# Sparse attention: the low parts of a finished pair one query block later on VectorE

## The chip, the cores and the metric

One core of a Trainium2 chip runs the whole program in one launch. The metric is the device time of that launch in microseconds (us); lower is better.

## The reference, cut to what matters

The reference is a chain of two transformer blocks over 512 tokens of width 1024. Nearly all of it stays out of this case. What matters is the mixer of the last layer, an attention of 12 heads (4 groups of 3) over 512 queries, with three branches that share the queries: over 31 compressed keys, over selected blocks of keys, and over a window. With 512 tokens all blocks are selected and the window covers all earlier keys, so that the two fine branches are causal attentions with their own keys and values:

```python
s_c = einsum('bgrqd,bgkd->bgrqk', qb, kc) + common_bias(d_c)
o_c = einsum('bgrqk,bgkd->bgrqd', masked_softmax(s_c, d_c >= 0), vc)
...
o = gb[..., 0:1] * o_c + gb[..., 1:2] * o_s + gb[..., 2:3] * o_w
...
h = h + jnp.concatenate([main, mo], axis=-1) @ w_out[i]
```

The kernel computes the dense products in fp32 from two parts of each operand: an upper part, rounded to the type that TensorE multiplies at full rate, and a low part, the rest. For the output projection (`@ w_out`), the attention's result is needed as xH (upper) and xL (low).

## The kernel before, in words

**Stages.** Each engine runs a hand-written list of stages in a fixed order: projections, the attention (`attend_pe`, `attend_dve`, `attend_act`), then the output projection `nsa_out` and the last feed-forward layer. Engines meet through counting semaphores alone.

**Pairs and blocks.** The 12 heads are worked off as 6 pairs. `items` (line 2467) lists 30 blocks: for each pair the coarse block over the compressed keys (t None), then the query blocks t = 0 to 3 of 128 queries, whose scores have 128(t + 1) columns. A block of t = 0 to 3 has two branches of two heads.

**The loop.** All three engines run m = 0 to 32, and each takes other blocks in one round:
- TensorE (`attend_pe`, L2553): the scores of block m (`scores_pe`; L2497 coarse, L2509 fine), which first wait until VectorE has the maxima of block m - 1 (`n_raw`); the turning (transposition, L881) of block m - 2, first branch; the product with the values of block m - 3 (`out_pe`, L2540 coarse, L2548 fine); the turning of the second branch.
- VectorE (`attend_dve`, L2643): the maxima of block m (`max_dve`: L2583 to L2592 coarse, L2600 and L2606 fine), which wait for the scores branch by branch; the scaling of block m - 1 (`scale_dve`, L2625 to L2639), which waits for its exponentials; and, when block m - 3 was the last of its pair, the low parts of that pair (`rest_dve`).
- ScalarE (`attend_act`, L2694): the copy of the turned block m - 2 (L2692), the exponentials of block m (`exp_act`, L2678), and, when block m - 3 was the last of its pair, the pair's upper parts (`upper_act`, L2712), which wait for all five products of the pair (`n_out`).

**The pair's result.** `out_pe` adds all five blocks of a pair up in one PSUM bank, bank 7 for even pairs and bank 2 for odd ones. `upper_act` copies its two halves (64 rows by 512 each) to xH and signals `x_hi`; `rest_dve` waits for that, subtracts xH from the bank into xL (L2659) and signals `x_ready`. `x_ready` is read by the coarse product of the pair after the next (L2538), which reuses the bank, and by `nsa_out`.

**The order on VectorE.** With the last block of a pair at index 5p + 4, the low parts stand in round 5p + 7: after the maxima of the next pair's block 1 and the scaling of its block 0, ahead of the maxima of its block 2. For the last pair this is round 32, where nothing else is left.

**Tables.** GpSimd loads the bias table of a later pair when `n_raw` tells that a pair's maxima are done (L2371). TensorE's clock is not set by the program.

Of the kernel before, what the change touches and what calls it, by code (L numbers as in the profile page):

```python
# [134 lines left out]
def build(nc, A, out):  # L135

    with ExitStack() as ctx:
        sems = {}

        def sem(name):  # L140
            if name not in sems:
                sems[name] = ctx.enter_context(nc.semaphore(name))
            return sems[name]
# [186 lines left out]
        def xbase(f):  # L330
            return sum(XFILL[:f])
# [1569 lines left out]
        def mem_out_dve(dve, l, base, place, hi):  # L1901

            dve.wait_ge(sem("m_out"), NROUND * (l + 1))
            for j in range(2):
                dve.wait_ge(sem("x_hi"), base + j + 1)
                nc.vector.tensor_tensor(place[:, j, :], bank[2 + j][:], hi[:, j, :], ALU.subtract)\
                  .then_inc(sem("x_ready"), 1)
# [558 lines left out]
        NPAIR = AH // 2  # L2466
        items = [(p, t) for p in range(NPAIR) for t in (None, 0, 1, 2, 3)]
# [3 lines left out]
        def pair_head(p, u):  # L2471

            return p + 3 * (p // 3) + 3 * u

        def lower_upper(half):

            return slice(64 * half, 64 * half + 64)
# [5 lines left out]
        def out_bank(p):  # L2483

            return bank[7 if p % 2 == 0 else 2]
# [157 lines left out]
        def attend_dve(dve):  # L2643
            for m in range(len(items) + 3):
                if m < len(items):
                    max_dve(dve, m)
                if m == 0:
                    mem_out_dve(dve, 1, xbase(9), xL[:, 6:8, :], xHf[:, 6:8, :])
                if 1 <= m <= len(items):
                    scale_dve(dve, m - 1)  # L2650
                if m >= 3 and items[m - 3][1] == 3:
                    rest_dve(dve, items[m - 3][0])

        def rest_dve(dve, p):
            for u in range(2):
                h = pair_head(p, u)
                f = lower_upper(h % 2)
                dve.wait_ge(sem("x_hi"), xbase(9) + 2 + 2 * p + u + 1)
                nc.vector.tensor_tensor(xL[f, h // 2, :], out_bank(p)[f, :], xHf[f, h // 2, :], ALU.subtract)\  # L2659
                  .then_inc(sem("x_ready"), 1)  # L2660
# [310 lines left out]
        def _(dve):  # L2971
# [74 lines left out]
            for k in range(KD):  # L3046
# [3 lines left out]
            dense_dve(dve, "nsa_q", evac_scaled(aq_place, rstd[:]),  # L3050
                      extra={(0, r): lambda r=r: mem_round_dve(dve, 1, r) for r in range(NROUND)})
            attend_dve(dve)
            dense_dve(dve, "nsa_out", residual(1.0))
            for k in range(KD):
# [65 lines left out]
```

## Time and profile before

| | |
|---|---|
| Time, median of 3 runs | 2518.57 us (2516.82 to 2520.32) |
| The profiled execution: its own time | 2519.59 us |
| its span, first to last instruction | 2517.8 us |
| Mean granted TensorE clock | 0.983 |
| Busy: TensorE matmul, VectorE, ScalarE, GpSimd | 97%, 53%, 38%, 6% of the span |
| DMA | 215.80 MB, mean 86 GB/s |

The profile is one execution. PE is TensorE's matmuls, PEld its weight loads, DVE is VectorE, ACT is ScalarE, POOL is GpSimd, SP is SyncE. A row of a timeline gives the start from the span's start and the length in us, the engine, the line of the kernel, the operation, what it writes and reads, and how many instructions are merged in it; in brackets stands the idle time of the engine before it and what ended that. The granted clock is a share of TensorE's full clock of 2.4 GHz. The ends of matmuls are modelled, so their starts are the firmer numbers.

### The profile page before, as it was taken

Reading aid. Unit: us, or ns where it says so; the run is one execution under the profiler, and the core shown is the slowest. Engines: PE = TensorE matmul, PEld = TensorE weight load, DVE = VectorE, ACT = ScalarE, POOL = GpSimd, SP = SyncE. Lnnn points to the kernel's source line nnn. Section 1 sums busy time; section 2 is a strip of 40 time slices with the busy share of each in tenths; the row PEclk is TensorE's granted clock in tenths of the full one; section 3 lists DMA queues with packets and bytes.
Section 4 is the critical chain, followed back from the end, with each engine's and each line's share of the span. In section 5 each row is a group of like instructions: output and inputs, shape, how many; then the busy total and the mean of one; then the engine's idle time right before and its main releaser. Section 6 shows DMA issues by size and latency. Waiting matters only on the chain.

```text
span 2517.8 us, 32093 instructions
## 1 busy us (share of the span) xinstructions
PE 2429.9 (97%) x12218; PEld 1972.6 (78%) x12218; DVE 1338.9 (53%) x2054; ACT 960.4 (38%) x1461; POOL 151.8 (6%) x130
## 2 busy tenths in 40 slices
PE   7999998998999999999899999999999888999999
PEld 6888886778878888887887788878887557888887
DVE  4344336665454343345785766643534873666633
ACT  4222226632243223235333533432324773433323
POOL 3000001013011000021000100000110000000001
PEclk9999999999999999999999999999999999999999
DMA  4333222220123332223122233332844102333322
GB/s 138 96 96 100 92 86 74 71 72 10 51 68 100 96 95 92 92 85 84 44 66 76 76 99 93 92 100 93 168 122 121 45 16 67 92 99 93 100 92 76
DMA packets 319121, 215.80 MB, mean 86 GB/s; under 512 B 49289, under 2 KB 302748, under 8 KB 319016
## 3 DMA queue, kind: packets, MB, share of 16 engines
q1 hardware_dynamic: 315752, 200.40, 27.7%
q0 software_dynamic: 3264, 13.94, 1.6%
q8 instruction: 72, 1.18, 0.2%
q14 instruction: 33, 0.27, 0.0%
HBM read 212.17 MB, written 8.44 MB: 88 GB/s over the span
## 4 chain that ended last, share of the span: by engine, by line
PE 85%; DVE 7%; ACT 5%; issue 2%; DMA 0%; POOL 0%; POOLq 0%; ACTq 0%; DVEq 0%
PE bank L521 17%; PE bank L522 16%; PE bank L523 16%; PE bank L708 6%; PE bank L707 6%; PE bank L706 6%; PE bank L881 1%; DVE wL L426 1%; DVE arena L2600 1%; ACT wH L390 1%; PE bank L2087 1%; PE bank L1569 1%; PE bank L2509 1%; PE bank L1583 1%; PE bank L1578 1%
## 5 line engine op out<-in xcount | busy, mean ns | idle before, releaser
L521 PE MATMUL bank<-xH,wH 128*128 128x512 f32 x1960 | 783.2, 400 | 21.0 <-DVE xL L780 10.0
L523 PE MATMUL bank<-xH,wL 128*128 128x512 f32 x1960 | 769.6, 393 | 0.0
L522 PE MATMUL bank<-xL,wH 128*128 128x512 f32 x1960 | 769.1, 392 | 0.0
L426 DVE TENSOR_TENSOR wL<-raw,wH 128x1024 fp32r<-128x1024 f32 (+1 forms) x359 | 449.5, 1252 | 535.4 <-ACT wH L390 534.9
L390 ACT ACTIVATE wH<-raw 128x1024 fp32r<-128x1024 f32 (+1 forms) x359 | 376.0, 1048 | 758.1 <-PE bank L523 342.8
L521 PEld LDWEIGHTS bank<-xH,wH 128*128 128x128 f32 x1960 | 369.4, 188 | 120.2 <-issue 27.9
L522 PEld LDWEIGHTS bank<-xL,wH 128*128 128x128 f32 x1960 | 369.9, 189 | 81.1 <-issue 4.8
L523 PEld LDWEIGHTS bank<-xH,wL 128*128 128x128 f32 x1960 | 369.2, 188 | 81.1 <-issue 1.0
L708 PE MATMUL bank<-g_hi,wL 128*128 128x512 f32 x704 | 280.9, 399 | 0.0
L706 PE MATMUL bank<-g_hi,wH 128*128 128x512 f32 x704 | 276.3, 393 | 1.2 <-DVE wL L426 1.2
L707 PE MATMUL bank<-g_lo,wH 128*128 128x512 f32 x704 | 277.4, 394 | 0.0
L2217 ACT ACTIVATE arena<-arena,par 128x512 f32<-128x512 f32 x88 | 63.6, 725 | 270.1 <-DVE arena L2249 270.1
L707 PEld LDWEIGHTS bank<-g_lo,wH 128*128 128x128 f32 x704 | 132.1, 188 | 34.1
L706 PEld LDWEIGHTS bank<-g_hi,wH 128*128 128x128 f32 x704 | 132.2, 188 | 34.0 <-DVE wL L426 2.5
L708 PEld LDWEIGHTS bank<-g_hi,wL 128*128 128x128 f32 x704 | 132.2, 188 | 30.5
L2249 DVE TENSOR_TENSOR arena<-bank,rstd 128x512 f32<-128x512 f32 x88 | 60.6, 691 | 86.6 <-PE bank L523 81.0
L733 ACT ACTIVATE arena<-arena 128x512 f32<-128x512 f32 x44 | 27.6, 631 | 173.8 <-DVE arena L740 173.8
L827 POOL TENSOR_TENSOR rstd<-sq 128x512 f32<-128x512 f32 x7 | 10.2, 1453 | 1290.7 <-ACT sq L790 1290.7
L742 DVE TENSOR_TENSOR arena<-bank,rstd 128x512 f32 (+1 forms) x44 | 30.3, 691 | 103.3 <-PE bank L523 103.3
L881 PEld LDWEIGHTS bank<-ident,arena 128*128 128x128 f32 (+3 forms) x402 | 46.0, 145 | 48.5 <-issue 34.7
L881 PE MATMUL bank<-ident,arena 128*128 128x128 f32 (+3 forms) x402 | 61.0, 292 | 22.8 <-DMA arena<-in_x 9.3
L740 DVE TENSOR_TENSOR arena<-bank,rstd 128x512 f32<-128x512 f32 x44 | 30.2, 691 | 85.6 <-PE bank L523 80.1
(337 smaller groups left out, 2679.0 us busy)
## 6 DMA issues: line engine op xcount, KB each, us to landing
raw<-in_ffn_w_in SPq DMA_DIRECT2D x88, 512.0 KB, 3.8
raw<-in_w_up SPq DMA_DIRECT2D x88, 512.0 KB, 3.8
raw<-in_ffn_w_out SPq DMA_DIRECT2D x44, 512.0 KB, 3.4
raw<-in_w_down SPq DMA_DIRECT2D x44, 512.0 KB, 3.5
raw<-in_w_mix_in SPq DMA_DIRECT2D x28, 512.0 KB, 3.8
raw<-in_w_kv_shared SPq DMA_DIRECT2D x12, 512.0 KB, 8.3
rel_wide<-rel_rows POOLq DMA_DIRECT2D x12, 512.0 KB, 10.9
arena<-rel_wide POOLq DMA_DIRECT2D x12, 448.0 KB, 4.2
```

The source lines that it names most:

```text
L390: nc.scalar.activation(wH[:, half_slot(s, i, j), 0:n], raw[:, k, 0:n], ACT.Copy).then_inc(sem("w_hi"), 1)
L426: nc.vector.tensor_tensor(wL[:, h, 0:n], raw[:, k, 0:n], wH[:, h, 0:n].bitcast(F32), ALU.subtract)\
L521: pe.matmul(o, wh, xa, start=a, stop=False)
L522: pe.matmul(o, wh, xb, start=False, stop=False)
L523: last = pe.matmul(o, wl, xa, start=False, stop=z)
L706: pe.matmul(bank[m][:], wh, gh, start=f == 0, stop=False)
L707: pe.matmul(bank[m][:], wh, gl, start=False, stop=False)
L708: last = pe.matmul(bank[m][:], wl, gh, start=False, stop=f == NF - 1)
L742: nc.vector.tensor_tensor(g[:, bass.ds(2 * i + t - 2, 1), :], one(bank[t][:]), one(rstd[:]), ALU.mult)\
L881: return pe.transpose(o, i, ident[0:k, 0:k])
L2217: nc.scalar.activation(cv[:, t, :], us[:, t, :], ACT.Copy, scale=conv_columns(s, i, t)[2])\
L2249: nc.vector.tensor_tensor(us[:, t, :], bank[t][:], rstd[:], ALU.mult).then_inc(sem("evac_dve"), 1)
```

## The change

The pair's low parts are made one round later: in round 5p + 8, that is after the maxima of the next pair's block 2 (its third fine block) and the scaling of its block 1, ahead of the maxima of its block 3. The last pair's low parts move behind the loop, where they follow the same instruction as before. No instruction, wait or signal is added or taken away.

```diff
--- before.py
+++ after.py
@@ -2648,8 +2648,9 @@
                     mem_out_dve(dve, 1, xbase(9), xL[:, 6:8, :], xHf[:, 6:8, :])
                 if 1 <= m <= len(items):
                     scale_dve(dve, m - 1)
-                if m >= 3 and items[m - 3][1] == 3:
-                    rest_dve(dve, items[m - 3][0])
+                if m >= 4 and items[m - 4][1] == 3:
+                    rest_dve(dve, items[m - 4][0])
+            rest_dve(dve, NPAIR - 1)
 
         def rest_dve(dve, p):
             for u in range(2):
```

## Rows read from the trace of the kernel before

**Rows 1.** Page, busy time of each engine, and the chain by engine.

```profile
PE 2429.9 (97%) x12218; PEld 1972.6 (78%) x12218; DVE 1338.9 (53%) x2054; ACT 960.4 (38%) x1461; POOL 151.8 (6%) x130
PE 85%; DVE 7%; ACT 5%; issue 2%; DMA 0%; POOL 0%; POOLq 0%; ACTq 0%; DVEq 0%
```

**Rows 2.** Attention stage: length, busy PE, PEld, DVE, ACT, POOL, PEclk, DMA, GB/s.

```profile
1942.00:2089.30 147.30, 123.07 (x1065) 82.06 (x1065) 112.20 (x459) 103.95 (x319) 4.48 (x9) 0.92 0.10 32
```

**Rows 3.** Waits, 1935 to 2092 us: total, times, longest.

```profile
DVE xL L2659 <- ACT xH L2712: 14.1, 6, 7.0
DVE arena L2600 <- PE bank L2509: 14.0, 13, 2.0
```

**Rows 4.** Timeline, low parts: start, length, engine, line, tiles [idle before, releaser].

```profile
2019.69 1.41 DVE L2659 TENSOR_TENSOR xL<-bank,xH 64x512 fp32r<-64x512 f32 x2 [1.37 <-ACT xH L2712]
...
2087.54 1.41 DVE L2659 TENSOR_TENSOR xL<-bank,xH 64x512 fp32r<-64x512 f32 x2 [7.01 <-ACT xH L2712]
```

**Rows 5.** Timeline of the third such place, PE and DVE.

```profile
2014.37 1.13 PE L2509 MATMUL bank<-arena 64*128 64x256 f32 x8
...
2015.26 0.42 DVE L2600 CUSTOM_DVE_ANT_0 arena<-bank,arena 128x256 f32<-128x256 f32 x1 [1.99 <-PE bank L2509]
...
2018.32 1.56 PE L2509 MATMUL bank<-arena 64*128 64x384 f32 x8
...
2021.13 0.56 DVE L2600 CUSTOM_DVE_ANT_0 arena<-bank,arena 128x384 f32<-128x384 f32 x1
2021.19 0.44 PE L881 MATMUL bank<-ident,arena 128*128 128x128 f32 x2
...
2023.19 3.38 PE L2509 MATMUL bank<-arena 64*128 64x512 f32 x8 [1.56 <-DVE col L2600]
...
2025.45 0.69 DVE L2600 CUSTOM_DVE_ANT_0 arena<-bank,arena 128x512 f32<-128x512 f32 x1 [0.46 <-PE bank L2509]
```

**Rows 6.** Timeline of DVE, waits in the maxima of block 3, other places.

```profile
1980.74 0.69 DVE L2600 CUSTOM_DVE_ANT_0 arena<-bank,arena 128x512 f32<-128x512 f32 x1 [0.16 <-PE bank L2509]
...
2048.60 0.69 DVE L2600 CUSTOM_DVE_ANT_0 arena<-bank,arena 128x512 f32<-128x512 f32 x1 [0.38 <-PE bank L2509]
...
2050.14 0.69 DVE L2600 CUSTOM_DVE_ANT_0 arena<-bank,arena 128x512 f32<-128x512 f32 x1 [0.23 <-PE bank L2509]
...
2073.20 0.69 DVE L2600 CUSTOM_DVE_ANT_0 arena<-bank,arena 128x512 f32<-128x512 f32 x1 [0.26 <-PE bank L2509]
```

**Rows 7.** Timeline round the coarse scores, pair 0 to 1, then 3 to 4.

```profile
1960.27 0.62 DVE L2583 TENSOR_TENSOR arena<-bank,arena 128x124 f32<-128x124 f32 x2
1960.40 0.88 PE L881 MATMUL bank<-ident,arena 128*128 128x128 f32 x6 [1.12 <-DVE arena L2639]
...
1969.63 0.43 DVE L2600 CUSTOM_DVE_ANT_0 arena<-bank,arena 128x256 f32<-128x256 f32 x1 [1.81 <-PE bank L2509]
...
2028.26 1.08 PE L2497 MATMUL bank<-arena 64*128 64x31 f32 x16
...
2030.10 0.62 DVE L2583 TENSOR_TENSOR arena<-bank,arena 128x124 f32<-128x124 f32 x2
2030.24 0.88 PE L881 MATMUL bank<-ident,arena 128*128 128x128 f32 x6 [0.90 <-DVE arena L2639]
...
2038.48 0.43 DVE L2600 CUSTOM_DVE_ANT_0 arena<-bank,arena 128x256 f32<-128x256 f32 x1 [1.99 <-PE bank L2509]
```

**Rows 8.** Table by stretches: clock, third from the end.

```profile
1945.00:1950.00 5.00, 4.28 (x22) 2.96 (x23) 4.01 (x25) 1.81 (x9) 0.00 (x0) 0.50 0.03 13
...
1961.20:1964.60 3.40, 3.40 (x25) 2.73 (x24) 2.82 (x10) 2.19 (x6) 0.00 (x0) 0.50 0.32 131
2022.60:2026.00 3.40, 2.81 (x8) 1.18 (x8) 2.81 (x13) 2.63 (x9) 0.00 (x0) 0.50 0.00 0
2029.50:2032.90 3.40, 2.59 (x28) 2.12 (x28) 3.19 (x13) 3.38 (x12) 0.00 (x0) 1.00 0.77 270
```

**Rows 9.** Timeline of DVE in the last pair, scale of block 3.

```profile
2078.24 0.17 DVE L2625 TENSOR_SCALAR col<-col 128x4 f32<-128x4 f32 x1 [1.61 <-ACT arena L2678]
```

## The prediction

> **What bounds the kernel now.** The page comes first: TensorE (PE) is busy for 97% of the span, and 85% of the chain that ended last is PE's [rows 1]. The change touches one stage only, the sparse attention, so I cut that stage out with the table by stretches: from 1942.0 to 2089.3 us it takes 147.3 us, with DVE (VectorE) busy for 112.2, PE for 123.1, ACT (ScalarE) for 104.0, at a mean granted clock of 0.92 [rows 2]. No engine is full there. The three hand work round: PE makes the scores of block m, DVE adds the table and takes their maxima, ACT takes the exponentials, DVE scales them, PE turns them, ACT copies them back, PE multiplies by the values. So I read who waits for whom in that stage: DVE waits 14.1 us for the upper parts in front of the low parts (L2659), in six places, and 14.0 us for scores [rows 3]. The last of the six is 7.01 us and lies behind the last pair [rows 4]; the change leaves it where it is. The other five sum to 7.1 us and are what can be won.
>
> Call the blocks of a pair c (coarse, t None), 0, 1, 2, 3, and let a prime mean the next pair. The pair's low parts now stand on DVE between scale(0') and max(2'). The timeline of one such place, the third of five, reads so [rows 4, 5]. DVE is done with scale(0') at 2019.69 - 1.37 = 2018.32. It waits 1.37 us for ACT's first upper part, makes two low parts of 0.69 us each (1.41 together), and starts max(2') only at 2021.13, though PE began those scores at 2018.32. PE then stands for 1.56 us before scores(3'), because these wait for max(2').
>
> **The change part by part.** No instruction is added or taken away: 12 subtractions, their 12 waits and 12 signals stay; no DMA is in what moves. The pair's low parts go behind max(2') and scale(1') for pairs 0 to 4, and for pair 5 they stay last.
>
> *The wait removed.* At its new place the low part finds x_hi long since raised, so its idle time is nothing. In its stead DVE waits for scores(2'). When are they there? For block 1' PE starts the scores at 2014.37 and DVE, which waits for the first branch, starts at 2015.26, 0.89 us later, on 256 columns in four passes of about 0.22 us [rows 5]. With 384 columns, the branch takes two passes of 0.11 us more: 0.89 + 0.22 = 1.11 us. So max(2') can start at 2018.32 + 1.11 = 2019.43, 1.70 us earlier than now, and DVE idles 1.11 instead of 1.37 us. Over five places: 7.1 - 5 x 1.11 = 1.55 us won. That is the step that makes the change small: most of the wait for ACT hid a wait for PE.
>
> *The work moved.* The 1.41 us of low parts now stand in front of max(3'). In the third place max(2') and scale(1') run from 2021.13 to 2025.45 - 0.46 = 2024.99 [rows 5]; 1.70 us earlier, scale(1') ends at 2023.3 and the low parts end at 2024.7. Scores(3') need the end of max(2') and PE's turn at 2021.19 + 0.44 = 2021.6, so they start near 2021.6 instead of 2023.19, and their first branch, which now takes 2025.45 - 2023.19 = 2.26 us at low clock [rows 5], is there at 2023.9 at the latest. Hence DVE goes from the low parts straight to max(3'), and the idle times now before and in max(3') vanish: 0.46 in that place, 0.16, 0.38 + 0.23 and 0.26 in others [rows 5, 6], 1.49 in sum. From max(3') on DVE has no idle time until max(1') of the next pair.
>
> *Who waits for the later low part.* Pair p's output bank is used again by pair p + 2 alone (L2538), a whole pair later, and xL is read by the output projection; neither comes near. No transfer of SP's or POOL's waits for it. On DVE max(3') is queued behind it, which is in the step above. I take nothing for the later signal; if one of its readers did wait, it would cost up to 1.41 us a place.
>
> *Sum of the direct effects:* 1.55 + 1.49 = 3.04 us won, in five places.
>
> *The clock.* PE's granted clock is 0.50 (1.2 instead of 2.4 GHz) in the stretch 2022.6 to 2026.0, right behind the 1.56 us in which PE stood [rows 8]; that is why the scores(3') of 512 columns take 3.38 us [rows 5]. Four of the five places have such a stretch, and it costs little there, the idle times of the last step. The change fills this gap, but moves it: scale(1') and ACT's exponentials of block 2' come 1.70 us sooner, so PE finishes turn(1'), the product of 0' and the next turn at least that much sooner, while the coarse scores of the next pair need the end of max(3'), which comes only 0.3 to 0.9 us sooner. In the third place PE now goes without a break into these scores (2028.26), waits 0.90 and starts turn(2') at 2030.24 [rows 7]. Afterwards it would stand some 1.5 us, make the coarse scores (1.08 us, of 31 columns each), stand about 1 us more, and only then go on. Of such a thin stretch the trace has one example: in pair 0, PE waits 1.12 us behind its coarse scores, and the clock is 0.50 from 1961.2 to 1964.6 [rows 7, 8]. There it is not free, since what follows is PE's own path (product, turn, scores(0'), product, turn, scores(1')), on which DVE waits 1.99 us even now. From the start of DVE's coarse sums to max(1'): 1969.63 - 1960.27 = 9.36 us in pair 0, against 2038.48 - 2030.10 = 8.38 us where the clock stayed up [rows 7]. The price is 0.98 us a pair. Bounds: nothing, if the clock stays up; and 3.4 us at half clock lose at most 1.7 us of work, of which 0.7 was slack in that example, so two such stretches running cost 3.4 - 0.7 = 2.7 us. I take 0.98, the row that shows it, four times (behind the last pair no coarse scores come): 3.9 us lost.
>
> The Trainium skill (TensorE: Matmul & The Clock Gate, HAM oscillation) says that waits between groups of matmuls put the clock back and that each next group then starts cold. The trace agrees in place and sign, as rows 8 show; if it held in none of the new gaps, the sum would be the 3.04 us of gain alone.
>
> *The end of the stage.* For the last pair max(3) comes about 0.6 us sooner; ACT's exponentials bound scale(3) there (DVE idle 1.61 us for them [rows 9]) and start from the same maxima, so the gain goes through to the output projection, whose first matmuls wait for the last low part. It is in the 3.04.
>
> *Total:* 3.9 - 3.04 = 0.9 us slower. The profiled execution was 2519.59 us (span 2517.8, 1.8 us around it), 1.0 us above the median of the runs shown, 2518.57; the sum is a difference and is set on the median: 2518.57 + 0.9 = 2519.5 us. Runs of this kernel differ by 3.5 us, and about 0.2% (5.0 us) is what a measurement can tell from no change.
>
> **Rivals.**
> 1. *The clock stays up.* The gap before scores(3') is filled and the two thin stretches around the coarse scores are too short to matter. For it: behind the coarse scores at 2028.26 the clock stayed at 1.00 in spite of 0.90 us of waiting [rows 7, 8]. Against: the new gap adds some 1.5 us just there, and the 1.12 us of pair 0 were enough. It gives 2518.57 - 3.04 = 2515.5 us. Chance 0.23.
> 2. *Slower: the clock stays down for two stretches running.* The mechanism is that of the forecast, at the same place, the path from turn(2') to scores(1'), but with the first low stretch begun before the coarse scores, so that PE does too little in it to get the clock back. It costs 2.7 us in each of four pairs: 10.8 - 3.04 = 7.8 us, 2526.4 us. It decides from (5.0 + 3.04)/4 = 2.0 us a pair. For it: the new thin stretch, some 3.7 us, is longer than any between two pairs now, and at the stage's start the clock was at 0.50 for 5 us and more [rows 8]. Against: the low stretches at 1961.2 and 2022.6 both ended after 3.4 us [rows 8]. Chance 0.12.
> 3. *More is won than I count.* Were scores(2') there when DVE is free, all five waits would go: 7.1 + 1.5 = 8.6 us, 2510.0 us. PE's product of the pair before ends at 2018.3 and stands in front; nothing in the change moves it. Chance 0.05.
> 4. *Nothing moves on the path.* If max(3') were bound by PE's turn and ACT's copies, the whole would stay at 2518.6 us. Against: ACT's waits in that place are for DVE. Chance 0.10.
>
> **How the numbers follow.** The forecast has 0.50, and its own range is 2517.5 to 2522 us (clock down in two to four of the pairs, 0.98 to 1.7 us each, and the scatter). The range for 8 in 10 takes in rival 1 with the scatter below and part of rival 2 above: 2514.3 to 2523.8 us. Faster by over 0.2% is below 2513.5: rival 3 and the tail of rival 1, 0.07. Slower by over 0.2% is above 2523.6: rival 2 and a little of the forecast, 0.13. Within: 0.80.
>
> **What would show it.** Right: five waits of L2659 for ACT gone, DVE idle 1.1 us before max(2') with PE's scores as the releaser; PE starting scores(3') without a wait; PE standing over 1 us before the coarse scores; granted clock 0.50 between those and scores(1') and no longer at scores(3'); the stage within 1 or 2 us of 147.3. Wrong: a clock of 1.00 through the stage (rival 1), or low stretches of 6.8 us (rival 2).

## The result, and the profile after

The changed kernel takes longer: 2528.74 us (median of 8 runs, 2521.10 to 2529.55) against 2520.09 us of the kernel before (8 runs side by side, 2516.30 to 2524.42). The ratio is 1.0032, with a 95% interval of 1.0020 to 1.0044, or 8.1 us (the two medians are 8.65 us apart). That is outside the range of the prediction (2514.3 to 2523.8) and near its second rival (2526.4). The profiled execution took 2529.54 us, with a span of 2527.8 us and a mean granted clock of 0.978 (before: 0.983).

Where the 8 us are, by the two profiles. The attention stage is taken from the maxima of the first coarse block to the first matmul of the output projection.

| | before | after |
|---|---|---|
| until the stage begins | 1942.4 us | 1944.4 us |
| the stage | 146.9 us | 151.5 us |
| of it, at granted clock 0.50 | 23.9 us | 44.4 us |
| projection to the end | 428.5 us | 431.8 us |

The first row is scatter: in second profiles of both kernels it was 1938.9 and 1939.4 us, while the other rows came out the same within 0.3 us (below). So the stage loses 4.6 us and the rest 3.3 us, 7.9 together. Of the 3.3, 1.6 are lost over the first 24 matmuls of the projection (7.2 us instead of 5.6) and 1.7 in the last 17 us of the program, where a stretch at clock 0.50 lasts 6.8 instead of 3.4 us.

The waits of the changed kernel in that stage (1935 to 2102 us; who for whom, total in us, times, longest) answer to [rows 3]:

```profile
DVE arena L2600 <- PE bank L2509: 24.6, 17, 1.8
DVE xL L2660 <- ACT xH L2713: 8.1, 1, 8.1
PE bank L2497 <- DVE col L2600: 7.0, 5, 1.7
```

The five waits of the low parts for ACT are gone, as the change means them to be; only the last pair's is left. What DVE waits for scores has grown from 14.0 to 24.6 us. PE waits 7.0 us ahead of the coarse scores, where the kernel before waited 0.5 us. PE's waits for DVE in other places have shrunk: ahead of the fine scores from 8.6 to 0.7 us, ahead of the turnings from 8.3 to 6.5 us. So PE waits less in sum than before, in other places.

The third of the five places, DVE's timeline after (start, length, engine, line, tiles, count [idle before, releaser]); it answers to [rows 4, 5]:

```profile
2024.42 0.56 DVE L2600 CUSTOM_DVE_ANT_0 arena<-bank,arena 128x384 f32<-128x384 f32 x1 [1.10 <-PE bank L2509]
...
2028.20 1.40 DVE L2660 TENSOR_TENSOR xL<-bank,xH 64x512 fp32r<-64x512 f32 x2
2029.63 0.69 DVE L2600 CUSTOM_DVE_ANT_0 arena<-bank,arena 128x512 f32<-128x512 f32 x1
...
2039.88 0.29 DVE L2600 CUSTOM_DVE_ANT_0 arena<-bank,arena 128x128 f32<-128x128 f32 x1 [1.68 <-PE bank L2509]
```

Up to 2029.63 all goes as it was meant to: 1.10 us of waiting ahead of the third block's maxima, low parts without a wait, the maxima of block 3 right behind them. Ten us later DVE waits 1.68 us for the scores of the next pair's block 0, where it had not waited before. PE's timeline of the same place says why:

```profile
2026.55 1.99 PE L2509 MATMUL bank<-arena 64*128 64x512 f32 x8
...
2032.21 1.91 PE L2497 MATMUL bank<-arena 64*128 64x31 f32 x16 [1.70 <-DVE col L2600]
2034.41 1.54 PE L881 MATMUL bank<-ident,arena 128*128 128x128 f32 x6 [0.29 <-DVE arena L2639]
2035.88 1.98 PE L2548 MATMUL bank<-arena 128*64 128x128 f32 x16
```

The scores of 512 columns now take 1.99 us (3.38 before, [rows 5]) and start without a wait. Then PE waits 1.70 us, and from the coarse scores on everything is slow: 1.91 us for what took 1.08, 1.54 for 0.88 ([rows 7]), 1.98 for 1.09. The table by stretches (length, busy PE, PEld, DVE, ACT, POOL with counts, granted clock, DMA, GB/s) answers to [rows 8]:

```profile
1984.50:1991.30 6.80, 6.12 (x42) 5.00 (x42) 5.26 (x17) 4.84 (x15) 0.81 (x2) 0.50 0.39 135
2008.40:2015.20 6.80, 6.36 (x44) 5.25 (x42) 5.46 (x18) 4.95 (x14) 1.06 (x2) 0.50 0.39 136
2032.30:2039.10 6.80, 6.51 (x44) 5.55 (x44) 5.60 (x20) 4.88 (x14) 1.06 (x2) 0.50 0.39 135
2056.20:2063.00 6.80, 6.58 (x44) 5.65 (x44) 5.69 (x20) 4.86 (x14) 0.00 (x0) 0.50 0.00 0
2080.10:2086.90 6.80, 4.65 (x28) 3.86 (x28) 4.17 (x15) 4.55 (x13) 0.00 (x0) 0.50 0.01 2
2097.10:2100.50 3.40, 3.40 (x10) 2.63 (x9) 0.01 (x1) 0.00 (x0) 0.00 (x0) 0.50 0.54 159
```

Behind each of the five places PE runs at 1.2 GHz for 6.8 us, and once more for 3.4 us at the start of the projection. The 44.4 us of the stage are these five and two stretches ahead of them that the kernel before has too, 6.8 us at the stage's start and 3.4 us behind the first pair's coarse scores.

### The profile page after: what moved, and what is told of

The parts are those of the page before. It is cut to its first block, busy times and chain, and to the rows that moved or that the text cites. A ratio compares the mean times of both kernels' runs of the same rounds, so it can differ in the third digit from the quotient of the medians.

```text
span 2527.8 us, 32093 instructions
## 1 busy us (share of the span) xinstructions
PE 2440.3 (97%) x12218; PEld 1986.2 (79%) x12218; DVE 1339.1 (53%) x2054; ACT 960.2 (38%) x1461; POOL 152.0 (6%) x130
## 4 chain that ended last, share of the span: by engine, by line
PE 86%; DVE 7%; ACT 4%; issue 2%; DMA 0%; POOL 0%; POOLq 0%; DVEq 0%; ACTq 0%
PE bank L521 16%; PE bank L522 16%; PE bank L523 16%; PE bank L708 6%; PE bank L706 6%; PE bank L707 6%; PE bank L881 2%; PE bank L2548 1%; DVE arena L2600 1%; DVE wL L426 1%; ACT wH L390 1%; PE bank L2087 1%; PE bank L1569 1%; PE bank L1583 1%; DVE xL L780 1%
## 5 line engine op out<-in xcount | busy, mean ns | idle before, releaser
L521 PE MATMUL bank<-xH,wH 128*128 128x512 f32 x1960 | 782.5, 399 | 23.4 <-DVE xL L780 11.9
L881 PE MATMUL bank<-ident,arena 128*128 128x128 f32 (+3 forms) x402 | 68.6, 318 | 21.3 <-DMA arena<-in_x 9.3
L881 PEld LDWEIGHTS bank<-ident,arena 128*128 128x128 f32 (+3 forms) x402 | 52.4, 160 | 45.3 <-issue 31.2
```

The source lines that it names most:

```text
L521: pe.matmul(o, wh, xa, start=a, stop=False)
L881: return pe.transpose(o, i, ident[0:k, 0:k])
```

## The experiments

All times are compared with runs of the kernel before on the same chip; its median was 2520.0 to 2520.3 us each time. Where two changed kernels are compared by their medians, these come from different groups of runs, and the difference of the ratios stands in brackets. "Coarse to coarse" is from the first to the sixth coarse maxima, five pairs long; the stage and the rest are as above; "low" is the time at clock 0.50 within the stage. These four columns come from one profile each, and one profile need not be the middle of all runs: in that of experiment 6 the stage and the rest are 3.8 us longer than in that of the kernel before, while the medians agree within 0.4 us.

| kernel | median us | ratio, 95% interval | coarse to coarse | stage | low | rest |
|---|---|---|---|---|---|---|
| before | 2520.09 | | 111.8 | 146.9 | 23.9 | 428.5 |
| before, again | 2515.91 (one) | | 111.7 | 146.7 | 23.9 | 428.6 |
| changed | 2528.74 | 1.0032 [1.0020, 1.0044] | 114.5 | 151.5 | 44.4 | 431.8 |
| changed, again | 2524.37 (one) | | 114.4 | 151.4 | 44.4 | 431.8 |
| 1 new order, coarse fillers | 2518.33 | 0.9993 [0.9984, 1.0002] | 108.3 | 143.9 | 13.7 | 431.7 |
| 2 new order, all fillers | 2517.02 | 0.9986 [0.9976, 0.9997] | 108.2 | 142.7 | 6.8 | 428.6 |
| 3 old order, all fillers | 2517.43 | 0.9989 [0.9981, 0.9998] | 108.4 | 143.1 | 3.4 | 429.2 |
| 4 old order, coarse fillers | 2517.81 | 0.9993 [0.9984, 1.0002] | 111.5 | 146.2 | 17.3 | 430.0 |
| 5 new order, fillers at the end | 2524.56 | 1.0017 [1.0008, 1.0026] | 114.5 | 150.4 | 37.5 | 428.7 |
| 6 low parts between | 2520.50 | 1.0002 [0.9993, 1.0011] | 111.5 | 147.4 | 23.9 | 431.8 |
| 7 one pair later | 2520.30 | 1.0006 [0.9997, 1.0015] | 111.8 | 147.8 | 27.3 | 430.1 |
| 8 new order, more fillers | 2516.90 | 0.9986 [0.9977, 0.9995] | 107.3 | 141.9 | 0.0 | 429.3 |
| 9 filler ahead only | 2520.31 | 0.9998 [0.9989, 1.0008] | 110.4 | 145.3 | 17.1 | 430.2 |
| 10 filler behind only | 2519.61 | 0.9995 [0.9984, 1.0007] | 110.2 | 145.8 | 20.5 | 430.2 |

**Is it the clock, or the order on VectorE?** Theory 1: the change makes PE thin round the next pair's coarse scores, the clock falls there, and PE's own path pays. The rival: the low parts in front of the maxima of block 3 cost the time themselves. They part when PE is given useless work in its waits: the order on DVE stays, the thin stretch goes.

```diff
+        def fill_pe(pe, done, widths):
+            pe.wait_ge(sem("x_ready"), xbase(9) + 2 + 2 * done)
+            for n in widths:
+                pe.matmul(out_bank(done + 1)[:, 0:n], ident[:], hT[:, 0, 0:n], start=True, stop=True, skip_group_check=True)
...
+                if m and m < len(items) and items[m][1] is None:
+                    fill_pe(pe, items[m][0] - 1, (512, 256))
                 if m < len(items):
                     scores_pe(pe, m)
+                if m and m < len(items) and items[m][1] is None:
+                    fill_pe(pe, items[m][0] - 1, (384,))
```

> The changed kernel, with extra matmuls of the identity by a resident tile (512 and 256 columns ahead of each coarse scores, 384 behind), written to the output bank that is free just then; they feed nothing. Theory 1, the low clock behind the coarse scores takes the time: granted clock 1.00 from there to block 1's maxima, DVE's wait before the maxima of block 0 gone from 1.7 us, coarse-to-coarse period down from 24.0 to about 22.2 us, and the time back to within 3 us of the kernel before (2517 to 2523), since the last pair's end is left as it is. Rival, the order on VectorE itself takes the time (low parts in front of the maxima of block 3): the fillers change nothing, 2526 to 2530.

2518.33 us, 10.4 us less than the changed kernel (9.8 by the ratios). PE's timeline at the matching place:

```profile
2020.87 1.46 PE L2556 MATMUL bank<-hT,ident 128*128 128x512 f32 x4
2022.73 1.08 PE L2497 MATMUL bank<-arena 64*128 64x31 f32 x16 [0.40 <-DVE col L2609]
2023.74 0.91 PE L2556 MATMUL bank<-hT,ident 128*128 128x384 f32 x2
2024.92 0.87 PE L881 MATMUL bank<-ident,arena 128*128 128x128 f32 x6 [0.28 <-DVE arena L2648]
2025.73 1.09 PE L2548 MATMUL bank<-arena 128*64 128x128 f32 x16
```

and the table by stretches, from the second pair to the last:

```profile
1958.20:2066.00 107.80, 102.05 (x909) 67.88 (x907) 88.16 (x366) 82.34 (x259) 3.20 (x6) 1.00 0.09 32
```

The same instructions on DVE in the same order, the clock at 1.00 throughout, the turning in 0.87 us and the product in 1.09 us as before. The four periods from the second coarse block on are 22.4 us each, where the changed kernel has 23.4, 24.15, 24.05 and 24.0. The rival (2526 to 2530) falls: with the same order on VectorE and the clock up, the loss is gone.

**With the last pair and the projection covered too**, by the same helper called ahead of the turnings of the last pair's blocks 2 and 3 and ahead of the projection:

```diff
+                if m == len(items):
+                    fill_pe(pe, NPAIR - 1, (512, 512, 512))
+                if m == len(items) + 1:
+                    fill_pe(pe, NPAIR - 1, (384,))
...
             attend_pe(pe)
+            fill_pe(pe, NPAIR - 1, (512, 384))
             dense_pe(pe, "nsa_out")
```

> As the one before, and with such matmuls also in the last pair (3 x 512 ahead of the turning of its block 2, 384 ahead of that of block 3) and ahead of the output projection (512 and 384). Theory 1: clock 1.00 from the second pair into the projection, 3 us less than the kernel with coarse fillers alone, and 3 to 5 us less than the kernel before: 2514 to 2517. Rival: no less than 2526.

2517.02 us: 3.2 us less than the kernel before beside it (3.5 by the ratio), at the lower end of the 3 to 5 expected, with an interval that leaves out 1. Against the version with the coarse fillers alone 3 us were expected. In the profiles the stage is 1.2 us shorter and the rest 3.1 us; the medians differ by 1.3 us only.

**The old order with the clock up**, with a filler of 512 columns ahead of the scores of block 3, one of 384 behind the coarse scores, and the ones at the end (384, 384, and 512 with 384).

> The kernel before, with such matmuls in its own gaps: 512 ahead of the scores of block 3, 384 behind the coarse scores, 384 twice in the last pair, 512 and 384 ahead of the projection. What the old order is worth with the clock up: the 1.49 us of waits in the maxima of block 3 go, and 1.0 us of the second pair: 2517 to 2518. The difference to the new order with all fillers is the direct effect of the order, 1.3 to 1.6 us by the five waits of 1.37 to 1.51 us that become 1.10 us. Rival (the order itself costs): the new order is 5 us or more behind this one.

2517.43 us, as expected. So with the clock up in both, the orders can't be told apart by time (2517.02 against 2517.43, intervals that overlap). The profiles can: the four later periods are 22.42, 22.40, 22.41, 22.34 us in the new order and 22.67, 22.70, 22.67, 22.61 in the old, and the last stretch 34.45 against 34.72. That is 1.35 us for the new order in five places; I had 1.55.

**Fillers where the clock was up anyway**: 256 columns ahead of and 384 behind the coarse scores of the old order.

> The kernel before, with 256 columns ahead of and 384 behind each coarse scores only. Control for what the fillers themselves do where the clock was up: within 2 us of the kernel before, the second pair's 1.0 us won at most. If the fillers won several us here, they would help by something other than the thin stretch that the change makes.

2517.81 us, and the interval of the ratio takes in 1. The stage is 0.7 us shorter. Fillers by themselves do little; the 10.4 us of the first experiment are not their doing. In this profile a low stretch of 3.4 us begins at 2089.2 us, 0.3 us ahead of the projection, as long as the one that the changed kernel has there, though neither order nor fillers of the last pair were touched.

**What the end costs**, the changed kernel with the fillers of the last pair and the projection alone.

> The changed kernel with the extra matmuls only in the last pair and ahead of the output projection, none round the coarse scores. It measures the term that the prediction left out. Theory: the low clock between the pairs stays (period 24.0 us), that of the last pair and of the projection's start goes; 3 to 4 us less than the changed kernel, about 2525. Rival: the last pair and the projection cost nothing by themselves, 2528 to 2529, and all of the loss lies between the pairs.

2524.56 us, 4.2 us less than the changed kernel (3.8 by the ratios; expected: 3 to 4), with the five periods unchanged at 114.5 us. The stage gives 1.1 us and the rest 3.1. The rival, that all of the loss lies between the pairs, falls: half of it lies behind them.

**Another place for the low parts**: also in the later round, but ahead of the scaling.

```diff
+                if m >= 4 and items[m - 4][1] == 3:
+                    rest_dve(dve, items[m - 4][0])
                 if 1 <= m <= len(items):
                     scale_dve(dve, m - 1)
-                if m >= 4 and items[m - 4][1] == 3:
-                    rest_dve(dve, items[m - 4][0])
```

> Low parts also in the later round, but ahead of the scaling of block 1 instead of behind it: the maxima of the third block still come 1.7 us sooner, while the scaling, and with it TensorE's turning and product, come 1.4 us later than in the changed kernel. If the thin stretch ahead of the coarse scores makes the low clock, its wait there shrinks from 1.70 to about 0.5 us and the low clock is rarer or shorter: period 22.4 to 23.4 us, time 2517 to 2522. If the later round itself is at fault, the time stays at 2527 to 2529.

2520.50 us, no difference from before. PE's timeline in the matching place:

```profile
2021.64 0.66 PE L881 MATMUL bank<-ident,arena 128*128 128x128 f32 x4 [1.24 <-DVE arena L2639]
...
2024.20 1.08 PE L2497 MATMUL bank<-arena 64*128 64x31 f32 x16 [0.73 <-DVE col L2600]
2026.40 1.54 PE L881 MATMUL bank<-ident,arena 128*128 128x128 f32 x6 [1.12 <-DVE arena L2639]
```

The wait for the maxima is split in two: 1.24 us now stand ahead of the turning and 0.73 ahead of the coarse scores, instead of 1.70 there. The clock still falls, but for 3.4 us at a time (23.9 us in the stage, as before), not 6.8. So the later round by itself doesn't cost the time. That the split of the waits makes the stretches shorter is read from this one profile; experiment 7 shows 3.4 us with the wait unsplit.

**One place alone**: only the third pair's low parts moved (the diff is against the changed kernel).

```diff
-                if m >= 4 and items[m - 4][1] == 3:
+                if m >= 3 and items[m - 3][1] == 3 and m < 32 and items[m - 3][0] != 2:
+                    rest_dve(dve, items[m - 3][0])
+                if m >= 4 and items[m - 4][1] == 3 and items[m - 4][0] == 2:
                     rest_dve(dve, items[m - 4][0])
```

> Only the third pair's low parts are moved, the others stay where the kernel before has them. Theory (low clock of 6.8 us behind the next coarse scores): one period of 24.0 us against 23.2, that is 0.8 to 1.6 us more than the kernel before, and 2520.5 to 2522. Rival (what comes behind each place adds up only when all are moved, by the phase of the low stretches): no difference from the kernel before.

2520.30 us; the interval of the ratio reaches from a gain of 0.8 us to a loss of 3.8, so the time decides nothing. The profile says more. The third pair's low parts lie between the fourth and the fifth coarse maxima, and the thin stretch that they make lies round the fifth. The period up to there is 22.41 us instead of 23.22, since the low stretch at the scores of block 3 is gone (0.81 won); the one behind it is 24.17 instead of 23.41 (0.76 lost). I had looked for the loss one period too early and had left out the gain. PE's row at the moved place, and the low stretch behind it:

```profile
2024.64 1.08 PE L2497 MATMUL bank<-arena 64*128 64x31 f32 x16 [1.70 <-DVE col L2600]
...
2026.60:2030.00 3.40, 3.16 (x22) 2.72 (x22) 3.19 (x12) 2.75 (x9) 0.00 (x0) 0.50 0.62 236
```

PE's waits here are those of the changed kernel, 1.70 us ahead of the coarse scores and 1.12 us behind them, but the low stretch begins 2.0 us behind the start of the coarse scores and lasts 3.4 us. In both profiles of the changed kernel and in that of experiment 5, without fillers round the coarse scores, it begins between 0.1 us ahead of that start and 0.5 us behind it, in 12 places of 12, and lasts 6.8 us. So the waits alone don't fix the length or the price; where the low stretch falls beside them goes with it. That is read from the profiles, one place against twelve; no run moved the stretch by itself.

**Both parts of the thin stretch.** The first filler alone, then the second alone, in the changed kernel.

> The changed kernel with extra matmuls (512 and 256 columns) only in the wait ahead of the coarse scores, the 1.70 us that the change makes; nothing behind them and nothing in the last pair. If this new wait is the cause, the pairs go back to what the kernel before had behind its coarse scores: low stretches at most now and then, periods of 22.4 to 23.4 us, 2518 to 2522. Rival: the waits behind the coarse scores weigh as much, and the periods stay near 24.

2520.31 us, as expected. In the profile low stretches of 3.4 us remain behind two of the coarse scores, with periods of 22.41, 22.41, 23.40 and 23.33 us.

> The changed kernel with extra matmuls (384 columns) only behind the coarse scores, in the wait that the kernel before had too. The wait that the change makes stays. If the new wait alone suffices for the low clock, periods stay between 23.4 and 24.0 and the time between 2522 and 2528; if the whole thin stretch is needed, they fall to 22.4 and the time to 2519.

2519.61 us, which fits the second of the two outcomes; of the periods (22.42, 23.12, 23.40, 22.34) only two do. With the wait of 1.70 us left in place, low stretches of 3.4 us remain behind three of the coarse scores. So with either wait covered no stretch of 6.8 us is left round the coarse scores in these two profiles, but low ones of 3.4 us are, and by experiment 7 a place with both waits open can have one of 3.4 us too.

**Is the pattern the program's?** Second profiles of both kernels.

> The changed kernel once more, for a second profile. If the low stretches are set by the program, they stand again behind all five places, 6.8 us each and 23.9 us apart, with the stage near 151.5 us; if the first profile was chance, some are missing and the time is nearer to 2521.

> The kernel before once more, for a second profile: low stretches of 3.4 us at the scores of block 3 in most places, the stage 145 to 147 us.

Both patterns came back. In the second profile of the changed kernel the low stretches lie at 1979.4, 2003.3, 2027.2, 2051.0 and 2074.9 us, 23.9 us apart and 6.8 us each, the stage is 151.4 us and the rest 431.8. In that of the kernel before, the stage is 146.7 and the rest 428.6, and the stretches are of 3.4 us at the scores of block 3 in four places. The times of these single executions, 2524.37 and 2515.91 us, are low by what stands ahead of the stage: it began at 1939.4 and 1938.9 us.

**A version faster than both**: all fillers, and three of 512 columns ahead of the first fine scores, where PE waits for the last low parts of the stage before.

```diff
+                if m == 1:
+                    for n in (512, 512, 512):
+                        pe.matmul(bank[7][:, 0:n], ident[:], hT[:, 0, 0:n], start=True, stop=True, skip_group_check=True)
```

> The new order with the extra matmuls everywhere, and three more of 512 columns ahead of the first fine scores, where TensorE waits 3.2 us and the clock is at 0.50 for 6.8 us in all kernels so far. Clock 1.00 through the whole stage, 1 to 2 us less than the kernel with all fillers: about 2515.5, and faster than both kernels.

2516.90 us, 0.9986 [0.9977, 0.9995]; about 2515.5 was expected. (The 6.8 us at 0.50 that the expectation gives all kernels at this place were 3.4 us in experiment 3.) The table by stretches, over the stage and the projection's start:

```profile
1943.00:2110.00 167.00, 155.54 (x1221) 105.42 (x1220) 120.61 (x467) 107.65 (x323) 4.45 (x9) 1.00 0.13 41
```

The clock is at 1.00 from end to end, and the stage is at its shortest, 141.9 us. It is faster than both kernels, but not measurably than the version with all fillers: the 0.8 us of the stage don't show in the medians of the times. (In seven of its 11 runs 2.0 to 2.9 us lie outside the span, where the others have 1.8; the medians of the spans are 2514.7 and 2515.3 us.)

## Why the prediction was wrong, point by point

Two terms failed: the price of a pair behind its coarse scores, 0.98 us, measured about 1.68; and the end of the stage with all that follows, put at nothing, where 4.2 us of the loss lie. The direct effects of the move came out near the 3.04 us that were forecast.

**The sum of the direct effects held.** Expected 1.11 us ahead of the third block's maxima, measured 1.10; no wait of the low parts for the first five pairs; scores of block 3 without a wait; maxima of block 3 straight behind the low parts. In the stage the clock costs the changed kernel, against the periods of 22.4 us with the clock up, 1.74 + 1.65 + 1.66 us behind the coarse scores of three pairs and 2.55 us in the last stretch (37.00 against 34.45), 7.6 us. The stage lost only 4.6, so 3.0 us were won: the 3.04 of the prediction. The part with the clock up, 1.55, is 1.35 in experiment 3. That the remainder meets 3.04 so closely is in part luck. By the periods of the kernel before against experiment 3, the low stretches at the scores of block 3 cost 2.04 us and not 1.49 (the 0.97 behind the first pair's coarse scores left out, which both kernels have), and the first period, ahead of all that was moved, is 0.35 us longer in the changed kernel's profile: 1.35 + 2.04 - 0.35 = 3.04.

**The low stretch was foreseen in place, not in length.** The prediction had PE stand some 1.5 us ahead of the coarse scores (1.70 measured), and the clock fall round them. It had DVE without idle time up to the maxima of block 1; in fact DVE waits 1.68 us ahead of block 0 too. It took the price from the one row of the trace before with such a stretch, 3.4 us long, 0.98 us ([rows 7, 8]). The stretches behind the changed places last 6.8 us and cost 1.74, 1.65 and 1.66 us, and I take their mean, 1.68, for the fourth, which lies in the last stretch: over four pairs 6.7 instead of 3.9. That is rival 2's mechanism, given 0.12 because the trace before showed only short stretches between pairs. But it showed them behind a thinner cause: there PE waited 1.12 us, while the change adds 1.5 us to this. The price of a cause that one has just made bigger should not be read off its smallest example. Nor was that example the only one, as the prediction says. The trace before has a second place with the same waits, 0.26 us ahead of the coarse scores at 2004.81 and 1.12 us behind them:

```profile
2007.01 0.88 PE L881 MATMUL bank<-ident,arena 128*128 128x128 f32 x6 [1.12 <-DVE arena L2639]
```

There the granted clock stayed at 1.00. The same waits had two outcomes in one trace, and the term needed a range from that.

**The end of the stage was costed at nothing.** "The gain goes through to the output projection" is the step that failed as a mechanism, beside the price of a pair, which was too small. In the last pair no coarse scores follow, and PE waits 3.82 us ahead of the turning of block 2, where it had waited 1.44:

```profile
2082.25 1.54 PE L881 MATMUL bank<-ident,arena 128*128 128x128 f32 x6 [3.82 <-DVE arena L2639]
```

The clock falls at 2080.1 for 6.8 us, and again at 2097.1, under the projection, whose matmuls fill PE. This cost 0.9 us in the stage (2.55 less one pair's 1.68; experiment 5 gives 1.1) and 1.6 us in the projection. In experiment 5 fillers in these waits alone give 4.2 us back. Only the part in the stage is tied to the longer wait. Ahead of the projection PE waits 2.42 us in the changed kernel and 2.41 in the one before, where the clock stayed up; and the profiles of experiments 1, 4, 6, 7, 9 and 10 have a low stretch of 3.4 us there as well, experiment 4 with the old order. It begins between 0.3 us ahead of the projection and 1.3 us behind its start. So the 1.6 us came to the changed kernel, in both its profiles, by where its low stretches fall; why they fall there was not tried.

**The last 1.7 us** lie in the end of the program, in a low stretch of 6.8 instead of 3.4 us, in both profiles of either kernel. Neither the order nor the fillers decide it: it lasts 6.8 us in experiments 1, 3, 6 and 8 as well, and 3.4 us in 2, 4, 5, 7, 9 and 10. Where it lasts 6.8 us it begins 12.2 to 14.3 us ahead of the last instruction, where it lasts 3.4 us 9.8 to 10.5 us. I take it for a shift of when the low stretches fall; that was not tried by itself and is open. (In experiments 3 and 8 the rest is 429.2 and 429.3 in spite of it, as they alone lack a stretch of 3.4 us that all others have 46 to 49 us behind the projection's start.)

Added up: 0.9 forecast, + 2.8 (four pairs) + 0.9 (last pair) + 1.6 (projection) + 1.7 (end) = 7.9 us, against 8.1 measured. The first three terms are the stage. The cause of the last two, 3.3 us, is open beyond the low clock itself.

**Rival 2 was right in kind and near in time (7.8 us), but by errors that offset each other:** it took 2.7 us a pair, where 1.7 were measured, and nothing behind the pairs, where 4.2 lie. Rival 1, the clock up, is what the fillers made true: 2515.5 forecast, 2518.33 and 2517.02 measured. Rivals 3 and 4 fall with the profile.

The rule of the Trainium skill that the prediction weighed (TensorE: Matmul & The Clock Gate, HAM oscillation: waits between groups of matmuls put the clock back) held in every changed place, by the stretches at 0.50 above. It would have put the last pair's 3.82 us into the sum. It did not hold for every wait: behind the 2.41 us ahead of the projection, and behind the 1.12 us of the row at 2007.01, the kernel before kept its clock at 1.00.

## What to carry to other kernels

A wait that is moved off a vector engine can reappear on TensorE next to another wait, and then costs more than itself, for its price is the clock of the work behind it. Before moving work, list TensorE's waits in order with the thin matmuls between them, before and after, up to the next dense stage, and look which path follows each: here 3.4 us of low clock at the scores of block 3, which other engines partly cover, cost 0.3 to 0.8 us (periods of the kernel before against experiment 3), the same on TensorE's own path 1.0 us (1.7 us where it lasted 6.8), and under a dense projection 1.6. The same waits had no low stretch, one of 3.4 us or one of 6.8 us in different places, so a price read off one place is a guess at the others. A few matmuls that feed nothing, put into such waits, held the clock; here they gave back 10 us in the changed kernel (12 with those at the end) and 3 in the one before.

## What the runs showed of the hardware that I had not expected

- The granted clock stayed at 0.50 for 6.8 us while PE was busy for 6.1 to 6.6 us of it (first four stretches above), and fell to 0.50 under the dense matmuls of the projection, 1.2 us after they began.
- In the changed kernel the coarse scores lay between a wait of 1.70 us and the one of 0.90 to 1.12 us that the kernel before had too (0.29 once they run slowly), and the clock fell in all four places. Fillers of 1.46 us in the first wait or 0.91 us in the second left low stretches of 3.4 us at most round the coarse scores, and in both waits none (one profile each).
- The pattern is regular: in both profiles of the changed kernel five low stretches 23.9 us apart, with pairs of 24.0 us. With one place moved (experiment 7) the stretch behind the same waits began 2.0 us behind the start of the coarse scores and lasted 3.4 us.
- Time ahead of the stage differs by 5.5 us between four profiles (1938.9 to 1944.4 us for the two kernels, whose programs are equal up to there), and by 3.5 and 5.0 us between the two profiles of one kernel. The runs of the kernel before scatter by 8.1 us (2516.30 to 2524.42); how much of that lies there is known for the profiled runs alone.
